# A two-layer diffusion backbone on one core: routing written in another order, and a down ring of nine slots

## What is computed

```
def moe_ffn(h, router, w_gu, w_d):
    logits = (h @ router).astype(jnp.float32)
    top_logits, top_idx = lax.top_k(logits, TOP_K)
    weights = jax.nn.softmax(top_logits, axis=-1)
    combine = jnp.sum(jax.nn.one_hot(top_idx, N_EXPERTS, dtype=jnp.float32) * weights[..., None], axis=-2)
    out = jnp.zeros(h.shape, jnp.float32)
    for e in range(N_EXPERTS):
        out = out + combine[..., e:e + 1] * swiglu(h, w_gu[e], w_d[e])
    return out.astype(h.dtype)
...
        x_lat = x_lat + m_lat[5] * rmsnorm(ffn(modulate(x_lat, norm_g[i, 2], m_lat[3], m_lat[4])), norm_g[i, 3])
```

## Time and profile before

| | us |
|---|---|
| median of 3 runs | 2488.49 |
| lowest, highest | 2486.59, 2490.86 |
| profiled execution | 2480.1 |
| its span | 2478.3 |
| turned tokens begin (L1136) | 1532.92 |
| first gather begins (L1209) | 1550.06 |
| last four gate/up units begin (L1186) | 2438.92 |

### The profile page before, as it was taken

The page is one execution under the profiler, slowest core; times in us unless marked ns, Lnnn a source line. Parts: engine busy times, 40 slices in busy tenths (PEclk is TensorE's granted clock), DMA queues, the critical chain, the costliest instruction groups (busy, mean ns, idle before and its releaser), DMA issues.

```text
span 2478.3 us, 43079 instructions
## 1 busy us (share of the span) xinstructions
PE 2267.4 (91%) x19363; PEld 1416.9 (57%) x19364; DVE 657.1 (27%) x1175; ACT 454.4 (18%) x771; POOL 48.5 (2%) x165
## 2 busy tenths in 40 slices
PE   6999879899999999897997997989999989999986
PEld 3474644344446877787877876433776333875332
DVE  1032450400000034776467753210000101000102
ACT  3134111200000116453424433000000000000001
POOL 0000000400000000000000000000000000000000
PEclk8999889999999999999999998999999989999998
DMA  7254101522223362102340025899998999999994
GB/s 260 85 184 164 60 1 51 191 98 68 85 68 119 138 233 94 46 4 74 126 153 4 5 80 222 330 407 407 406 359 302 407 407 407 398 321 339 407 407 196
DMA packets 181951, 502.60 MB, mean 203 GB/s; under 512 B 9571, under 2 KB 73381, under 8 KB 175621
## 3 DMA queue, kind: packets, MB, share of 16 engines
q1 hardware_dynamic: 180148, 494.27, 53.5%
q0 software_dynamic: 1616, 5.54, 0.7%
HBM read 498.72 MB, written 1.05 MB: 202 GB/s over the span
## 4 chain that ended last, share of the span: by engine, by line
PE 40%; DMA 6%; SPq 6%; DVE 4%; issue 2%; ACT 1%; DVEq 0%; ACTq 0%
PE banks L968 8%; PE banks L1224 7%; PE banks L1243 7%; PE banks L1186 7%; DMA ring_arena<-in_moe_w_gu 6%; SPq L495 4%; PE banks L735 3%; SPq L502 2%; PE banks L1197 1%; PE banks L1209 1%; PE banks L1120 1%; PE banks L1179 1%; PE banks L915 1%; DVE ring_arena L1987 1%; PE banks L928 1%
## 5 line engine op out<-in xcount | busy, mean ns | idle before, releaser
L1186 PE MATMUL banks<-ring_arena 128*64 128x448 f32 x1536 | 320.2, 567 | 46.6 <-DMA ring_arena<-in_moe_w_gu 46.6
L735 PE MATMUL banks<-ring_arena 128*128 128x256 f32 (+1 forms) x1024 | 314.9, 466 | 15.4 <-DVE ring_arena L1793 9.3
L872 PE MATMUL banks<-ring_arena 128*128 128x512 f32 x704 | 305.4, 597 | 6.4 <-ACT ring_arena L1308 6.1
L735 PEld LDWEIGHTS banks<-ring_arena 128*128 128x128 f32 x1024 | 195.5, 192 | 134.2 <-issue 102.0
L1224 PE MATMUL banks<-ring_arena 128*64 128x512 f32 (+1 forms) x896 | 251.5, 605 | 7.0 <-DVE ring_arena L2204 7.0
L1186 PEld LDWEIGHTS banks<-ring_arena 128*64 128x64 f32 x1536 | 110.4, 142 | 237.3 <-issue 220.6
L968 PE MATMUL banks<-ring_arena 64*64 64x128 f32 (+1 forms) x6144 | 203.6, 256 | 35.9 <-DVE ring_arena L1992 19.1
L872 PEld LDWEIGHTS banks<-ring_arena 128*128 128x128 f32 x704 | 134.7, 192 | 176.3 <-issue 175.2
L968 PEld LDWEIGHTS banks<-ring_arena 64*64 64x64 f32 x6144 | 191.1, 135 | 42.7 <-issue 29.2
L1224 PEld LDWEIGHTS banks<-ring_arena 128*64 128x64 f32 (+1 forms) x896 | 90.5, 149 | 153.0 <-issue 151.9
L1243 PEld LDWEIGHTS banks<-ring_arena 128*64 128x64 f32 x3584 | 171.8, 137 | 9.4 <-issue 9.2
(11 more groups left out here) (340 smaller groups left out, 2006.8 us busy)
## 6 DMA issues: line engine op xcount, KB each, us to landing
ring_arena<-in_moe_w_gu SPq DMA_DIRECT2D x256, 896.0 KB, 16.3
ring_arena<-in_moe_w_d SPq DMA_DIRECT2D x112, 1024.0 KB, 17.1
ring_arena<-in_mod_w SPq DMA_DIRECT2D x48, 1024.0 KB, 6.7
ring_arena<-in_ff_w_gu SPq DMA_DIRECT2D x22, 1024.0 KB, 5.1
ring_arena<-in_ff_w_d SPq DMA_DIRECT2D x22, 1024.0 KB, 4.9
ring_arena<-in_rw_w_rkv SPq DMA_DIRECT2D x20, 1024.0 KB, 5.3
ring_arena<-in_gla_w_in SPq DMA_DIRECT2D x12, 1024.0 KB, 5.4
ring_arena<-in_gla_w_out SPq DMA_DIRECT2D x4, 1024.0 KB, 6.4
```

The costliest lines, as they stand in the source:

```text
L735: ins = T.matmul(b[:, 0:width], w[:, k, j * P:j * P + P], src[:, k, :], start=(k == 0), stop=(k == KT - 1))
L872: ins = T.matmul(ps[4 * (p % 2) + 2 * ab + j][:, :], w[:, k, j * P:j * P + P], H2[:, k, :], start=(k == 0), stop=(k == KT - 1))
L1186: ins = T.matmul(ps[2 * half][slots_at(h, CH), 0:BLOCK], XG[:, 2 * kp + kk, 0:CH], w[:, kk, BLOCK * h:BLOCK * h + BLOCK], start=(kp == 0 a ...
```

## The change

It does three things.

1. **Order of routing.** TensorE turns the residual stream first, ahead of the wait for `H3` and into banks 0 to 3; then come the logits; then the turned tokens, into banks 6 and 7 alone, so that the third and the fourth set of four wait for ScalarE's copies; then the counts; then the gain. Its waits for the copies of the residual and the gain move from ahead of the first gather to behind it. ScalarE copies the tokens, takes the exponentials, and copies the residual and the gain after that. `GAIN_ROW` lies in `std` and `rstd` now, which frees `sq`.
2. **Order on VectorE.** After the counts come the positions, then both `PG`, and only then the exponentials' steps and both `PW`. In every item the two `PG` now stand ahead of the two `PW`, and the gather waits for `PG` alone.
3. **Nine down slots.** Slot 7 is the place of `H3`, slot 8 the scratch tile `sq`/`ntmp`. SyncE fills seven slots as before, then waits until `H3` has been turned, fills two more and goes on. The loop for further items uses the first seven slots only.

```diff
-WD_UNITS, WD_RING, WD_SLOT = FE // SEG, 7, 2 * D
+WD_UNITS, WD_RING, WD_FIXED, WD_SLOT = FE // SEG, 9, 7, 2 * D
...
-        GAIN_ROW, GAIN_DIAG = sq[:, :], at(15600, KT, P)
+        GAIN_ROW, GAIN_DIAG = [std[:, :], rstd[:, :]], at(15600, KT, P)
...
+        wd_slots += [at(2048, WD_SLOT), sqn[:, :]]
+        wd_main = [len(range(i, WD_UNITS * NE, WD_RING)) for i in range(WD_RING)]
+        def wd_slot(n, u, first):
+            return (WD_UNITS * n + u) % WD_RING if first else u % WD_FIXED
+        def wd_free(n, u, first):
+            if first:
+                return WD_UNITS * n + u + 1
+            return WD_RING + WD_UNITS * n + max(u - WD_FIXED + 1, 0)
...
             gate_up(0, 0, range(GU_RING))
-            down(0, 0, range(WD_RING))
+            down(0, 0, range(WD_FIXED))
+            sp.wait_ge(S["h_tm"], 4)
+            down(0, 0, range(WD_FIXED, WD_RING))
...
-                pe.wait_ge(S["pg"], 4 * n + 4)
+                pe.wait_ge(S["pg"], 4 * n + 2)
...
+                if first and n == 0:
+                    pe.wait_ge(S["res_out"], 4)
+                    pe.wait_ge(S["gain_out"], 2)
...
             for n in range(4):
                 act.wait_ge(S["h_tm"], n + 1)
-                C.copy(HTM[:, n // 2, 512 * (n % 2):512 * (n % 2) + 512], ps[n][:, :]).then_inc(S["h_tm_out"], 1)
+                C.copy(HTM[:, n // 2, 512 * (n % 2):512 * (n % 2) + 512], ps[6 + n % 2][:, :]).then_inc(S["h_tm_out"], 1)
+            act.wait_ge(S["sel"], 1)
+            C.activation(EXL[:, :, :], EXL[:, :, :], ACT.Exp).then_inc(S["ex_out"], 1)
```

More of the change, by code:

```diff
@@ L84 @@
         + [("gu", 8 * g + 4 + kp) for kp in range(4)]] + [("wd", u) for u in GROUP_DOWN[GROUPS - 1]]
-assert GU_UNITS % GU_RING == 0 and WD_UNITS % WD_RING == 0
+assert GU_UNITS % GU_RING == 0 and WD_UNITS % WD_FIXED == 0
 def hybrid_backbone(nc, A, out):
@@ L253, in hybrid_backbone, with wd_landed @@
         gu_slots = [ring_arena[:, GU_SLOT * i:GU_SLOT * i + GU_SLOT] for i in range(GU_RING)]
-        wd_slots = [arena[:, 17664 + WD_SLOT * i:17664 + WD_SLOT * i + WD_SLOT] for i in range(WD_RING)]
+        wd_slots = [arena[:, 17664 + WD_SLOT * i:17664 + WD_SLOT * i + WD_SLOT] for i in range(WD_FIXED)]
+        wd_slots += [at(2048, WD_SLOT), sqn[:, :]]
+        wd_main = [len(range(i, WD_UNITS * NE, WD_RING)) for i in range(WD_RING)]
+        def wd_slot(n, u, first):
+            return (WD_UNITS * n + u) % WD_RING if first else u % WD_FIXED
+        def wd_landed(n, u, first):
+            if first:
+                return 16 * ((WD_UNITS * n + u) // WD_RING + 1)
+            per_item = WD_UNITS // WD_FIXED
+            return 16 * (wd_main[u % WD_FIXED] - per_item * NE + u // WD_FIXED + 1) + 16 * per_item * n
+        def wd_free(n, u, first):
+            if first:
+                return WD_UNITS * n + u + 1
+            return WD_RING + WD_UNITS * n + max(u - WD_FIXED + 1, 0)
         S = {n: sem(n) for n in (
@@ L266, in hybrid_backbone @@
             "sums kam rates e3 e2 keys_b ident_a ident_z vt vt_out st_zero u_ready head_sets b_mm b_out ln_b mean_mm mean_sub var_sq var_mm var_std var_rcp spread gate_mm o_in "
[L267 to L268 removed]
+            "h_tm h_tm_out rt_in logits ex_out sel pos route pg xg xg_out sil hid_tm hid_t hh pwt pwt_out yd_out sc sc_out res_t res_out gain_diag gain_mm gain_out fin_ss fin_ms fin_std gu_used wd_used "
+            "v_chain s_chain p_chain out_c stored").split()}
         def mod(layer, j, k, sg):
@@ L486, in _, with gate_up @@
             gu, wd = A["moe_w_gu"][0], A["moe_w_d"][0]
-            def gate_up(e, n, units):
+            def gate_up(e, n, units, first=True):
                 for u in units:
@@ L495, in gate_up, with down @@
                     sp.dma_start(gu_slots[u % GU_RING].rearrange("p (k n) -> p k n", k=2), src).then_inc(gu_in[u % GU_RING], 16)
-            def down(e, n, units):
+            def down(e, n, units, first=True):
                 for u in units:
                     src = wd[e, SEG * u:SEG * u + SEG, :].rearrange("(k p) n -> p k n", p=P)
-                    sp.wait_ge(S["wd_used"], WD_UNITS * n + u + 1)
-                    sp.dma_start(wd_slots[u % WD_RING].rearrange("p (k n) -> p k n", k=2), src).then_inc(wd_in[u % WD_RING], 16)
+                    sp.wait_ge(S["wd_used"], wd_free(n, u, first))
+                    i = wd_slot(n, u, first)
+                    sp.dma_start(wd_slots[i].rearrange("p (k n) -> p k n", k=2), src).then_inc(wd_in[i], 16)
             def number(n):
@@ L1128, in _ @@
             T.transpose(ps[5][:, 0:P], ident[:, :], ident[:, :]).then_inc(S["wd_used"], WD_RING)
+            pe.wait_ge(S["post_done"], 4 * KT)
+            for q in range(4):
+                for k in range(4 * (q % 2), 4 * (q % 2) + 4):
+                    ins = T.transpose(ps[q][:, (k % 4) * P:(k % 4) * P + P],
+                                      X[:, k, SEG + q // 2 * P:SEG + q // 2 * P + P], ident[:, :])
+                ins.then_inc(S["res_t"], 1)
             pe.wait_ge(S["h_ready"], 5 * KT)
             pe.wait_ge(S["consts"], 10)
[L1133 to L1137, removed]
             pe.wait_ge(S["rt_in"], 16)
@@ L1148, in _ @@
                 for k in range(4 * (q % 2), 4 * (q % 2) + 4):
[L1149 to L1158, removed]
+                    ins = T.transpose(ps[6 + q % 2][:, (k % 4) * P:(k % 4) * P + P],
+                                      H3[:, k, q // 2 * P:q // 2 * P + P], ident[:, :])
+                ins.then_inc(S["h_tm"], 1)
+            pe.wait_ge(S["sel"], 2)
             T.matmul(ps[5][:, 0:NE], BEFORE[:, :], SEL[:, 0, :], start=True, stop=True)
@@ L1164, in _ @@
             ins.then_inc(S["pos"], 1)
-            pe.wait_ge(S["h_tm_out"], 4)
-            pe.wait_ge(S["res_out"], 4)
-            pe.wait_ge(S["gain_out"], 2)
+            pe.wait_ge(S["gain_diag"], 1)
+            for h in range(2):
+                pe.wait_ge(S["h_tm_out"], h + 3)
+                T.matmul(ps[6 + h][:, :], ones[:, :], GAIN_DIAG[:, 4 * h:4 * h + 4, :],
+                         start=True, stop=True).then_inc(S["gain_mm"], 1)
             def scatter(n, q, cap):
@@ L2118, in _, with gather_slots, scatter_slots, slots_of @@
                 ins = Vv.tensor_scalar(EXL[:, t, :], LOG[:, t, :], MX[:, t:t + 1], None, ALU.subtract)
-            ins.then_inc(S["ex_in"], 1)
+            ins.then_inc(S["sel"], 1)
             Vv.tensor_scalar(SEL[:, :, :], SEL[:, :, :], 1.5, None, ALU.is_lt).then_inc(S["sel"], 1)
-            dve.wait_ge(S["sel"], 1)
+            dve.wait_ge(S["pos"], 1)
+            link(Vv.scalar_tensor_tensor(RK0[:, :, :], ps[5][:, 0:2 * NE].rearrange("p (a b) -> p a b", a=2), 1.0,
+                                         SEL[:, :, :], ALU.add, ALU.mult))
+            link(Vv.tensor_scalar(RK[:, :, 0:1], RK0[:, :, 0:1], -1.0, None, ALU.add))
+            link(Vv.tensor_copy(COUNTS, ps[5][:, 2 * NE:3 * NE]))
+            def gather_slots(pos, cap):
+                for t in range(2):
+                    Vv.tensor_scalar(PG[:, t, 0:cap], SLOTS[:, 0:cap], pos[t], None, ALU.is_equal).then_inc(S["pg"], 1)
+            def scatter_slots(pos, wt, cap):
+                for t in range(2):
+                    Vv.tensor_scalar(PW[:, t, 0:cap], SLOTS[:, 0:cap], pos[t], wt[t], ALU.is_equal, ALU.mult).then_inc(S["pg"], 1)
+            def slots_of(pos, wt, cap):
+                gather_slots(pos, cap)
+                scatter_slots(pos, wt, cap)
+            gather_slots([RK[:, t, 0:1] for t in range(2)], CAPS[0])
             dve.wait_ge(S["ex_out"], 1)
@@ L2126, in _ @@
             link(Vv.tensor_tensor(CMB_EXPERT[:, :, :], EXL[:, :, :], MX[:, :].unsqueeze(2).to_broadcast([P, 2, NE]), ALU.mult))
-            dve.wait_ge(S["pos"], 1)
-            link(Vv.scalar_tensor_tensor(RK0[:, :, :], ps[5][:, 0:2 * NE].rearrange("p (a b) -> p a b", a=2), 1.0,
-                                         SEL[:, :, :], ALU.add, ALU.mult))
-            link(Vv.tensor_scalar(RK[:, :, 0:1], RK0[:, :, 0:1], -1.0, None, ALU.add))
-            link(Vv.tensor_copy(COUNTS, ps[5][:, 2 * NE:3 * NE]))
[L2134 to L2138, removed]
+            scatter_slots([RK[:, t, 0:1] for t in range(2)], [CMB_EXPERT[:, t, 0:1] for t in range(2)], CAPS[0])
             by_rank, by_expert = PLACE_ROW.unsqueeze(2).to_broadcast([P, NE, NE]), SLOTS[:, 0:NE].unsqueeze(1).to_broadcast([P, NE, NE])
```

17 lines of the change are left out of this document (8 added, 9 removed).

## The result

The changed kernel took 2469.43 us (median of 4 runs, 2466.33 to 2472.46), the kernel before 2487.54 (4 runs, 2484.55 to 2490.86). The profiled execution of the changed kernel took 2472.46 us against 2480.1 before, only 7.6 less. The two numbers don't agree, and the first thing to find out was which of them tells of the change.

What follows compares the result with a forecast made beforehand. Weight stream and TensorE were taken to bound the kernel in turns, the end hanging on the stream. Routing 6.7 plus two down slots 5.15 gave 11.85 us saved: 2476.6 us from the median 2488.49, range 2472.5 to 2484.

Steps and rivals of the forecast that it cites:

- The stream lost 11.9 us ahead of item 0: Start of item 0: weight stream idle with full rings, 8.6 + 3.3 = 11.9 us lost; the change can't gain more.
- The routing starts the first products 6.7 us earlier: Routing: the new order takes 10.4 us in place of 17.1 up to the first gather, so 6.7 us earlier.
- The first refill follows the first products by 3.2 us as before: Start of item 0: first products near 1550.4, first refill issued 3.2 us later at 1553.6, before the stream runs dry.
- A down slot is worth 2.58 us, once, at the end: Down ring: each added unit is 2.58 us of stream, two 5.15, reaching TensorE only at the last gate/up units.
- The rival that each heavy item gives it again: Heavy items: a fuller ring behind each gives 5.15 us again, 22.1 saved, 2466.3 us; chance 5 in 100.
- The stream thins with more units out: Light items: rate falls with 17 units out in place of 15; at 395 GB/s 7.7 us slower, 2496.2; 4 in 100.
- The sum's base: Whole kernel: the 11.85 us saving taken from the median of 2488.49 us, giving 2476.6.
- The whole 11.85 reaches the end: End of item 7: last gate/up units land 11.85 us early, at 2427.07, and the kernel's end gains all of it.
- theory B: Follow-up experiments' theory: the change gives some 6 us more, in a place that the two traces don't show.

## Why the prediction was wrong, point by point

**The stream lost 11.9 us ahead of item 0, and that caps what both halves can give.** The runs bear it out. Order and slots alone close 8.4 and 5.4 us of it, 13.8 together, and shorten the part by 8.4 and 4.7 us. The changed kernel closes all 11.9 and no more, and its part is 10.4 to 12.0 us shorter. What is closed doesn't always arrive in full: with eight slots 8.5 us were closed and 6.7 arrived, and where the rest goes wasn't settled.

**The routing starts the first products 6.7 us earlier.** The size came out right (24.2 to 17.5) by luck. The prediction had the gather start 6.7 us earlier and stay slow; it started 3.1 us earlier (14.0 us after `H3` in place of 17.1) and ran fast, which the prediction had kept for its high end. The logits were put at 3.63 us and took 7.01; the gather was put at 7.06 and took 3.52. The forecast took durations from rows at whatever clock they had been run at, and moved them to places where the clock was another. The logits' 3.63 us had been measured at a mean granted clock of 0.94; it was the transposes ahead of them that ran at 0.53. In the new order nothing stands between the wait for `H3` and the logits, and they ran at 0.50, the 1.2 GHz level. The two errors cancelled: 3.4 against 3.5.

**The first refill follows the first products by 3.2 us as before.** Wrong: 1552.86 - 1551.17 = 1.7 in the changed kernel, since the first unit runs at the high clock too. It fits that the order alone gave 8.4 and not 6.7. With both halves it made no difference to the stream, because of the cap.

**A down slot is worth 2.58 us, once, at the end.** Borne out by the slots alone: no shift until the last four gate/up units, then 4.7 us (5.15 forecast). On top of the new order, which leaves only 3.5 us of loss, the two slots gave 2.0 to 3.5. The wait ahead of the last four units was 0.40 and 0.43 us in two traces of the changed kernel, where 0.4 was worked out; in the third there was none. With eight slots it was 2.96, and with seven 5.49 in the old order but 3.01 in the new one, so the number of slots alone doesn't set it.

The rival that each heavy item gives it again is out for down slots. It was expected of gate/up slots: 4.5 us at each of three places, 20 with the order. Against the order alone, the two gate/up slots are 3.3 and 3.6 us ahead at item 2, 4.7 and 5.4 at item 5, 7.1 and 7.9 at the end of the part. The first step agrees with the cap, for the order leaves just 3.5 us to gain there. Behind each heavy item something is gained again, but less than 4.5: about 1.6, then 2.5. Down units that come later in the queue don't explain it, since none was waited for; what takes the rest wasn't settled.

**The stream thins with more units out.** It doesn't: the changed kernel has 407 GB/s at the start of item 0, and in a long light stretch:

```profile
1564.00:1754.00 190.00, 172.95 (x855) 69.38 (x856) 19.56 (x56) 6.45 (x13) 0.00 (x0) 0.93 1.03 407
```

**The sum's base.** This is the step that failed: "Against the median of 2488.49, which lies 8.4 higher, the same saving gives 2476.6." The saving was carried over from a trace to a median of three runs, as if those three stood for the kernel. They were on its long side: the medians of 17 and 23 later runs of the kernel before are 2483.47 and 2483.89. From there the same 11.85 us lead to 2471.6 to 2472.0, and a range set in the same way would have held the measured 2469.43. And the range gave 4 us to the scatter of runs, read from three runs that lay 4.3 apart, where more of them reach over 20.

**"The whole 11.85 reaches the end."** Not in the traces. Behind the last gate/up product the last down units took 1.5 to 3.0 us more than before (table), a term that the sum put at nothing.

**What stays open.** The mixture's part shortened by 10.9 us (mean of three traces against 914.8). Whole traced executions shortened by less, 7.7 us (mean 2471.0 against 2478.7), since `H3` was there 2.4 us later on average and what follows the part took 0.8 us longer. The medians lie 13.5 and 14.3 us apart in the two larger series, so some 6 us of them aren't in any trace. The four traced executions of the kernel before took 2475.05 to 2480.1, all of them below the median of its timed runs; those of the changed kernel took 2470.03 to 2472.46, all above its own. An execution of the kernel before that took 2490 us was never traced. The list of runs holds a hint: among the 23 of the kernel before, the longest (2495.47) had a mean granted clock of 0.951 and the shortest (2474.61) one of 0.960, and the means over the runs were 0.955 before and 0.958 with the change in one series, 0.956 and 0.957 in the other. What lowers the clock in the long ones, and whether the change takes some of it away, isn't shown. So theory B is refuted only where it puts a slow stretch into the mixture (914.7 to 915.1 us in all four traces); a gain outside of it is neither shown nor excluded.

## What to carry to other kernels

Ask of a ring which kind of unit its consumer waits for, and put spare memory there: two down slots were worth 4.7 us in the old order, once at the end, and 2.0 to 3.5 on top of the new order; the same memory as gate/up slots was worth 7.1 and 7.9 on top of the new order. Two edits that close the same gap don't add up: at the start of the stage, the idle time of the stream (11.9 us) was the most that both could give. Take a duration along with the granted clock that it was measured at. And before a saving of half a per cent is carried over to a median, see how far the kernel's own runs lie apart: here 11 to 21 us between executions, while the stage under study took the same time within 0.5 us in four traces.

## What the runs showed of the hardware

The granted clock of TensorE moves whole steps of routing by a factor of two, also where they are bound by weight loads: 32 matmul instructions of 8 columns, with weight loads busy all the time, took 3.5 to 3.8 us in the old order and 7.01 in every version with the new one. The step that pays is the one that stands first behind the wait for `H3`. These are the transposes and the logits of the kernel before (columns as in the earlier trace rows):

```profile
1532.92:1536.49 3.57, 3.56 (x19) 3.57 (x19) 0.45 (x1) 1.76 (x3) 0.00 (x0) 0.53 1.04 409
1536.49:1540.12 3.63, 3.63 (x34) 3.63 (x33) 0.00 (x0) 0.58 (x1) 0.00 (x0) 0.94 1.01 403
```

and these the two halves of the logits, then the transposes, of the changed kernel:

```profile
1533.65:1537.00 3.35, 3.35 (x16) 3.35 (x16) 0.45 (x1) 0.00 (x0) 0.00 (x0) 0.50 1.03 407
1537.00:1540.66 3.66, 3.66 (x19) 3.66 (x19) 0.00 (x0) 0.00 (x0) 0.00 (x0) 0.50 1.02 407
1540.66:1544.30 3.64, 3.58 (x16) 2.82 (x15) 3.17 (x16) 1.78 (x4) 0.00 (x0) 0.50 1.03 410
```

The Trainium skill, TensorE: Matmul & The Clock Gate, What's actually happening, says that the low clock is the default and that activity lifts it. The rows agree in that the first work behind the wait starts low and the clock is high later on. But in the old order it was high after 3.6 us of transposes, and in the new one it was still at 0.50 after 7.01 us of logits and most of 3.6 us of transposes: busy time alone doesn't tell when it rises.

Whether the gain's products got the low clock (3.45 us or 1.82) changed from one trace to the next with no edit to the order. The last down units took 8.57 to 10.08 us in three traces of one and the same changed kernel, but 7.09 in all four of the kernel before. A stream of weights, by contrast, ran at 407 GB/s in the light items of every trace, and the part of the kernel before that it mostly bounds repeated within 0.5 us (within 1.6 us in the changed kernel).
